# Decoder trunk on one core: seeded banks at feed-forward ends, the last tile on ScalarE, later gains

## What is computed

```python
h = LN(ALPHA * h + 0.5 * swiglu(h, ffn_a))     # gate and up 1024 x 2816, down 2816 x 1024
h = LN(ALPHA * h + mixer(h))                   # three groups of heads, one projection in, one out
h = LN(ALPHA * h + 0.5 * swiglu(h, ffn_b))
# swiglu(x) = (silu(x @ w_gate) * (x @ w_up)) @ w_down;  LN(x) = (x - mean) * rsqrt(var + eps) * g + b
```

## Time and profile before

| | |
|---|---|
| runs | 1899.64, 1900.06, 1900.58 us |
| median | 1900.06 us |
| the profiled execution's own time | 1899.35 us |
| its span, first to last instruction | 1897.6 us |
| mean granted TensorE clock | 0.998 of full speed |
| busy: TensorE, VectorE, ScalarE, GpSimd | 98%, 74%, 39%, 11% |

### The profile page before, as it was taken

How to read it: one execution, slowest core, us unless ns; L and a number is a source line. 1 busy time by engine, 2 the same in 40 slices (tenths; PEclk the granted TensorE clock), 3 DMA queues, 4 the chain that set the end, 5 groups by cost and what they waited for, 6 DMA issues and landing times.

```text
span 1897.6 us, 25000 instructions
## 1 busy us (share of the span) xinstructions
PE 1867.6 (98%) x9121; PEld 1572.7 (83%) x9121; DVE 1411.4 (74%) x2059; ACT 741.0 (39%) x1114; POOL 217.0 (11%) x247
## 2 busy tenths in 40 slices
PE   7999999999999999999999999999999999999998
PEld 6888888889888888888888888888888888888886
DVE  7877877952676878787897777777536688777777
ACT  5332333434554423333253242423455543424243
POOL 2000000153323000000100000003343220000001
PEclk9999999999999999999999999999999999999999
DMA  5222223236742222222313222223557323222221
GB/s 215 100 111 88 111 88 133 91 119 179 207 115 90 111 88 111 88 111 88 133 69 131 89 111 88 111 111 107 153 156 210 89 83 115 111 88 111 88 111 45
DMA packets 43747, 215.95 MB, mean 114 GB/s; under 512 B 8756, under 2 KB 11252, under 8 KB 20008
## 3 DMA queue, kind: packets, MB, share of 16 engines
q1 hardware_dynamic: 40808, 199.30, 29.7%
q0 software_dynamic: 2880, 15.90, 3.6%
HBM read 197.23 MB, written 17.93 MB: 113 GB/s over the span
## 4 chain that ended last, share of the span: by engine, by line
PE 90%; DVE 5%; issue 2%; ACT 1%; DMA 1%; POOL 1%; SPq 0%; ACTq 0%; DVEq 0%; POOLq 0%
PE psum L1011 80%; PE psum L1216 5%; PE psum L1313 2%; DVE res L1540 1%; PE psum L1303 1%; PE psum L1042 1%; PE psum L1291 1%; DVE st L1557 1%; DVE negm L1898 1%; DVE xlo L1496 0%; DMA gbc<-in_gb_col 0%; PE psum L1415 0%; PE psum L1242 0%; POOL rstd L609 0%; ACT psum L919 0%
## 5 line engine op out<-in xcount | busy, mean ns | idle before, releaser
L1011 PE MATMUL psum<-xhi,whiA 128*128 128x512 f32 (+1 forms) x768 | 287.4, 374 | 4.9 <-DVE xlo L1496 4.9
L1011 PE MATMUL psum<-xlo,whiA 128*128 128x512 f32 (+1 forms) x768 | 285.9, 372 | 0.0
L1011 PE MATMUL psum<-xhi,wloA 128*128 128x512 f32 (+1 forms) x768 | 285.8, 372 | 0.0
L1011 PE MATMUL psum<-xhi,whiB 128*128 128x512 f32 x704 | 273.9, 389 | 0.0
L1011 PE MATMUL psum<-xlo,whiB 128*128 128x512 f32 x704 | 273.9, 389 | 0.0
L1011 PE MATMUL psum<-xhi,wloB 128*128 128x512 f32 x704 | 273.9, 389 | 0.0
L1011 PE MATMUL psum<-whiD,hl 128*128 128x512 f32 x768 | 264.0, 390 | 2.0 <-DVE wloD L1473 2.0
L799 ACT ACTIVATE s<-psum 128x512 f32<-128x512 f32 x40 | 23.9, 598 | 540.7 <-PE psum L1011 540.6
L1651 DVE SCALAR_TENSOR_TENSOR res<-psum,res 128x1024 f32<-128x1024 f32 x120 | 146.7, 1222 | 82.1 <-PE psum L1011 82.1
L1651 DVE SCALAR_TENSOR_TENSOR nat<-psum,nat 128x1024 f32<-128x1024 f32 x144 | 175.8, 1221 | 26.3 <-PE psum L1011 26.3
L1011 PEld LDWEIGHTS psum<-xhi,whiA 128*128 128x128 f32 x768 | 145.4, 189 | 32.4 <-DVE xlo L1496 6.0
(11 more groups left out here) (230 smaller groups left out, 3520.5 us busy)
## 6 DMA issues: line engine op xcount, KB each, us to landing
rawA<-in_a_w SPq DMA_DIRECT2D x62, 1024.0 KB, 6.3
rawB<-in_b_w SPq DMA_DIRECT2D x54, 1024.0 KB, 4.8
rawD<-in_d_w SPq DMA_DIRECT2D x46, 1024.0 KB, 4.7
stacks<-hl SPq DMA_DIRECT2D x192, 64.0 KB, 1.7
whiD<-stacks POOLq DMA_DIRECT2D x10, 768.0 KB, 6.4
wloD<-stacks POOLq DMA_DIRECT2D x10, 768.0 KB, 5.9
gbr<-in_gb_row SPq DMA_DIRECT2D x6, 1024.0 KB, 8.4
stacks<-wloD SPq DMA_DIRECT2D x48, 64.0 KB, 1.7
```

The lines of the kernel that those rows point to most:

```text
L1011: ins = t_.matmul(out_, a_, b_, start=(start and k == 1), stop=(stop and k == n), skip_group_check=check)
```

## The change

1. At the end of a feed-forward stage ScalarE copies tiles 0 and 1 of `res` into banks 4 to 7 (the seeds), and the products of the first four output halves are added on top of them (start is off). VectorE adds nothing there: it takes the statistics from the banks, and ScalarE normalises tiles 0 and 1 from the banks. The other four halves go to banks 2, 3, 2, 3 and are added to `res` as before. So that the banks need no factor, h is scaled by 0.5 as it is split. `y_free` counts four additions at such an end (`freed`).
2. Fold 4 is cut in two: the two additions that finish tiles 0 and 1 stand ahead of the split of D, the two others where all four stood.
3. After a feed-forward stage tiles 0 and 1 are turned into banks 4 to 7, and tiles 2 and 3 too.
4. At all five joints ScalarE normalises tile 3, behind its split of B; VectorE's `last_tile` inside `turn` goes.
5. At all five joints VectorE does three half-chunks ahead of the last addition and three behind it (BEGUN = 6), and only then the last statistics. With 4, its half-chunks 6 and 7, the last subtraction and the low part of B follow the aggregate directly.
6. In the first seven-product of a stage the gains of tiles 1 to 3 all move behind the low part of the sums of D (tlo).
7. The output stage swaps the two groups of banks.

```diff
-OUT_BANKS = [(0, 1, 2, 3), (4, 5, 6, 7)]
+OUT_BANKS = [(4, 5, 6, 7), (0, 1, 2, 3)]
...
+BEGUN = 6
+SEED_BANKS = (4, 5, 6, 7)
+SEEDED = 4
+FFN_BANK = [4, 5, 6, 7, 2, 3, 2, 3]
+Y_ADDS = (8 - SEEDED, 8, 8 - SEEDED)
...
+        def freed(y):
+            l, i = divmod(y, Y_ALL)
+            return 4 + l * sum(Y_ADDS) + sum(Y_ADDS[:i])
+        def after_ffn(q):
+            return q > 0 and q % 3 != 2
+        def half_banks(q, h):
+            return SEED_BANKS if after_ffn(q) else HALF_BANKS[h]
...
                         act.wait_ge(y_done, y * 8 + AHEAD)
                         split("B", b_fill)
+                        act.wait_ge(nmr_ok, NT * q + NT)
+                        a.activation(nat[:, NT - 1, :], res[:, NT - 1, :], ACT.Identity, bias=nmr[:, NT - 1:NT],
+                                     scale=rstd[:, NT - 1:NT]).then_inc(zd_ok, 1)
...
+                    if after_ffn(q) and t < 2:
+                        a.activation(nat[:, t, :].rearrange("p (a n) -> p a n", a=2), psum[:, 4 + 2 * t:6 + 2 * t, :], ACT.Identity,
+                                     bias=nmr[:, t:t + 1], scale=rstd[:, t:t + 1]).then_inc(za_ok, 1)
...
-                    a.activation(hhi["A"], h32["A"], ACT.Copy).then_inc(hhi_ok["A"], 1)
+                    a.activation(hhi["A"], h32["A"], ACT.Copy, scale=0.5).then_inc(hhi_ok["A"], 1)
+                    act.wait_ge(fold_ok, (2 * l + f) * 8 + 6)
+                    for t in range(2):
+                        a.activation(psum[:, 4 + 2 * t:6 + 2 * t, :], res[:, t, :].rearrange("p (a n) -> p a n", a=2),
+                                     ACT.Copy).then_inc(seed_ok, 1)
...
+                if after_ffn(q) and h == 1:
+                    pe.wait_ge(y_free, freed(y))
...
+                        if after_ffn(q) and h == 0:
+                            if (t, i) == (0, 2):
+                                pe.wait_ge(za_ok, 3 * q + 2)
...
-                    if n == 0:
-                        pe.wait_ge(y_free, y * 8 + o + 1)
-                    ins = product(bank[4 + o % 4][:, :], [(stat(t), w(slot, off + hf * 512, 512))],
-                                  start=(n == 0), stop=(n == 1))
+                    if n == 0 and o < SEEDED:
+                        pe.wait_ge(seed_ok, y // Y_ALL * 4 + (2 if y % Y_ALL else 0) + t + 1)
+                    elif n == 0 and o >= 6:
+                        pe.wait_ge(y_free, freed(y) + o - 5)
+                    ins = product(bank[FFN_BANK[o]][:, :], [(stat(t), w(slot, off + hf * 512, 512))],
+                                  start=(n == 0 and o >= SEEDED), stop=(n == 1), check=o < SEEDED)
...
-                        if q and h == 0 and c == 5:
-                            dve.wait_ge(rstd_ok, NT * q + NT)
-                            last_tile(q)
...
+                    if o < seeded:
+                        dve.wait_ge(y_done, y * 8 + o + 1 + AHEAD)
+                        summed = bank[FFN_BANK[o]][:, :]
+                    else:
+                        dve.wait_ge(y_free, freed(y) + o - seeded + 1)
+                        summed = res[:, t, hf * 512:hf * 512 + 512]
+                    v.bn_stats(st[:, t, hf, :], summed).then_inc(st_ok, 1)
...
+                if seeded:
+                    for o in range(4):
+                        stats(o)
...
+                stats(late - 1)
+                for c in range(3):
+                    half_chunk(q + 1, 0, c)
+                for o in range(late, 8):
+                    add(y, o)
+                for c in range(3, BEGUN):
+                    half_chunk(q + 1, 0, c)
+                for o in range(late, 8):
+                    stats(o)
...
+                    fold(4)
                     split("D", l * D_ALL + f * D_FFN2 + i)
...
-                    v.tensor_tensor(hlo["A"], h32["A"], f32(hhi["A"]), ALU.subtract).then_inc(h_ok["A"], 1)
-                    fold(4)
+                    v.scalar_tensor_tensor(out=hlo["A"], in0=h32["A"], scalar=0.5, in1=f32(hhi["A"]), op0=ALU.mult,
+                                           op1=ALU.subtract).then_inc(h_ok["A"], 1)
+                    fold(5)
...
+                    elif k == 4:
+                        dve.wait_ge(m_free, (q + 1) * SEVENS * 7 + AHEAD)
+                        add_to(c12, m6, 3)
+                        add_to(c11, m1)
                     else:
                         add_to(m7, m5)
-                        dve.wait_ge(m_free, (q + 1) * SEVENS * 7 + AHEAD)
-                        add_to(c12, m6, 3)
-                        add_to(c22, m7, 5)
-                        add_to(c11, m1)
+                        add_to(c22, m7, 7)
...
-                    if begin:
-                        gain(1)
-                        gain(2)
...
-                    if begin:
-                        gain(3)
                     split("D", d)
                     dve.wait_ge(thi_ok, n + 1)
                     v.tensor_tensor(tlo, tsum, f32(thi[:, :]), ALU.subtract).then_inc(tlo_ok, 1)
+                    if begin:
+                        for t in range(1, NT):
+                            gain(t)
```

More of the change, by code:

```diff
@@ L749, in normalise @@
                     act.wait_ge(nmr_ok, NT * q + t + 1)
-                    a.activation(nat[:, t, :], res[:, t, :], ACT.Identity, bias=nmr[:, t:t + 1],
-                                 scale=rstd[:, t:t + 1]).then_inc(za_ok, 1)
+                    if after_ffn(q) and t < 2:
+                        a.activation(nat[:, t, :].rearrange("p (a n) -> p a n", a=2), psum[:, 4 + 2 * t:6 + 2 * t, :], ACT.Identity,
+                                     bias=nmr[:, t:t + 1], scale=rstd[:, t:t + 1]).then_inc(za_ok, 1)
+                    else:
+                        a.activation(nat[:, t, :], res[:, t, :], ACT.Identity, bias=nmr[:, t:t + 1],
+                                     scale=rstd[:, t:t + 1]).then_inc(za_ok, 1)
             def ffn(l, f):
@@ L784, in last_pair @@
                         a.activation(hhi["B"][:, h * 256:h * 256 + 256], h32["B"][:, h * 256:h * 256 + 256],
-                                     ACT.Copy).then_inc(hhi_ok["B"], 1)
+                                     ACT.Copy, scale=0.5).then_inc(hhi_ok["B"], 1)
                 def gather(n, k):
@@ L1032, in turn_z @@
                     for i in range(NT):
[L1033 to L1036 removed]
+                        b = half_banks(q, h)[i]
+                        if after_ffn(q) and h == 0:
+                            if (t, i) == (0, 2):
+                                pe.wait_ge(za_ok, 3 * q + 2)
+                        elif not after_ffn(q) and t == 0 and (b >= 6 or h == 0 and b >= 4):
+                            pe.wait_ge(y_free, freed(y) + b - 7)
                         elif t == 0 and h == 1:
@@ L1561, in stats @@
                         v.bn_aggr(mv[:, t, :], st[:, t, :, :].rearrange("p a n -> p (a n)")).then_inc(mv_ok, 1)
[L1563 to L1570, removed]
+                if seeded:
+                    for o in range(4):
+                        stats(o)
+                else:
+                    for o in range(4):
+                        add(y, o)
+                        if o >= 1:
+                            stats(o - 1)
+                    stats(3)
                 for o in range(4, late):
-                    add(y, o, scale)
+                    add(y, o)
                     if o >= 5:
                         stats(o - 1)
[L1575 to L1579, removed]
-                        add(y, o, scale)
-                        half_chunk(q + 1, 0, 2 + o - late)
-                    for c in range(2 + HELD, 4):
-                        half_chunk(q + 1, 0, c)
-                    for o in range(late, 8):
-                        stats(o)
-                else:
-                    stats(7)
+                if ends:
+                    stats(7)
+                    return
+                stats(late - 1)
+                for c in range(3):
+                    half_chunk(q + 1, 0, c)
+                for o in range(late, 8):
+                    add(y, o)
+                for c in range(3, BEGUN):
+                    half_chunk(q + 1, 0, c)
+                for o in range(late, 8):
+                    stats(o)
             def ffn(l, f):
-                turn(3 * l + 2 * f, l * B_ALL + f * B_FFN2, 4 if l + f else 0)
+                turn(3 * l + 2 * f, l * B_ALL + f * B_FFN2, BEGUN if l + f else 0)
                 if (l, f) == (0, 0):
@@ L1613, in last_pair @@
                         dve.wait_ge(hhi_ok["B"], n * 2 + h + 1 + AHEAD)
-                        v.tensor_tensor(hlo["B"][:, t], h32["B"][:, t], f32(hhi["B"][:, t]), ALU.subtract).then_inc(h_ok["B"], 1)
+                        v.scalar_tensor_tensor(out=hlo["B"][:, t], in0=h32["B"][:, t], scalar=0.5, in1=f32(hhi["B"][:, t]),
+                                               op0=ALU.mult, op1=ALU.subtract).then_inc(h_ok["B"], 1)
                 def gain(t):
```

31 lines of the change are left out of this document (18 added, 13 removed).

## The result

The changed kernel takes **1906.81 us** (median of 8 runs, 1903.85 to 1909.68) beside 1900.16 for the kernel before. The ratio is 1.0036, with a 95% interval of 1.0025 to 1.0047: slower, and 2.8 us above the upper end of the predicted range. One of the eight executions of the kernel before took 3119.34 us; it counts in the median and not in the ratio, which is of fast runs alone. The profiled execution is one of the quicker ones, 1905.41 us with a span of 1903.7. Its span is 6.1 us above that of before, where the prediction's sum said 1.6.

A forecast was written before the change was run, and what follows sets the result against it. TensorE, busy 98% of the span, was taken as the bound; -0.62 + 0.5 + 0.6 + 1.96 - 0.87 = +1.6 us gave 1900.9 profiled, 1901.6 as a median, with a range of 1892 to 1904.

The forecast's parts named there:

- the end of the joint after a feed-forward stage: Tile 3's transposes and seventh chunk of x: chunk at 376.15 against 375.95, loss 0.2 us, three times.
- last pair: Last two products of h in a stage: second half of h comes later, cost 0.12 us each, 0.5 for four.
- The forecast's mechanism: At the joints GpSimd's last operation asks 0.14 us after VectorE's split of B starts, and waits until 373.92.
- The mixer joints: Two joints after a mixer: chunk at 607.33 against 606.35, loss 0.98 us each, 1.96 in all.
- The tail: End of the kernel: last aggregate at 1887.6 against 1888.47, gain 0.87 us.
- The first products: First stage: the wait for wloD goes, ScalarE's first gather is late next; gain 0.62 us, once.
- The seeds: Two ScalarE copies per stage, taken at 1.05 us each, in idle time; no cost even at 2.0.
- The race the other way: Rival, chance 0.20: after a feed-forward stage GpSimd asks before the split of B; 1.8 us gained three times, 1895.6.
- The whole hold by GpSimd: Rival, chance 0.15: GpSimd's rstd holds VectorE's reads for its whole length, so nmr precedes the split of B; 1892.6.
- The cast that I held against this rival: Sign against GpSimd holding reads: a cast at 366.59 kept its 0.29 us during rstd at 366.43.
- The lost handover: Rival, chance 0.10: waiting GpSimd can't get between VectorE's instructions, rstd waits for the split's end; 0.7 more per joint, 1905.1.
- My slower rival: At five joints VectorE's queue wins over GpSimd's older request; 0.7 us more each, 1905.1, chance 0.10.

The follow-up runs named there:

- run 2: Changed kernel plus nine products nobody reads ahead of TensorE's wait for tile 3 at all five joints; 1901.31 us, ratio 1.001.
- run 12: Changed kernel plus the nine unread products at the two joints after a mixer only; 1904.28 us, ratio 1.0027.
- run 11: Changed kernel plus the nine unread products at the three joints after a feed-forward stage only; 1902.27 us, ratio 1.002.
- run 1: Changed kernel plus one wait: VectorE starts its split of B at a joint only when nmr is done; 1891.08 us, ratio 0.9955.

## Why the prediction was wrong

**The step that failed is the end of the joint after a feed-forward stage**: "ScalarE 374.0 to 375.25, the tile's transposes at 375.3, and the chunk 0.85 later". The 0.85 is a duration at 2.4 GHz, and I carried it behind a wait of 2.7 which the kernel before has nowhere at a joint. The granted clock was never asked for there; it stood at 1.00 in all I read. Nothing in the sum, the rivals or the range has a term for it. In the profiled execution it costs 1.39, 1.57 and 1.54 at the three joints, measured against run 2 (4.50). Joint and last pair together cost 0.21, 0.18 and 0.18 in run 2, where the prediction had 0.32, so without the clock the sum was near. The 4.50 are as large as the missing 4.5 in part by luck: the rest of the ledger misses too, -0.97 at the start against +1.10 in the mixers and +0.25 at the end.

The timed runs pay more: their mean clock is 0.995 or 0.996 in seven of eight, the profiled one's is 0.997, and one fall is 3.41 us at half speed in 1904, 0.0009 of the mean. Run 2, with the same tail, has 0.999 or 1.000 in all ten. The mean is a rough counter, though: one execution of run 12 shows 0.972 at 1906.29 us, only 2 above its median. Run 2 measures the term in the timed runs, 5.5 us (4.9 by the ratios), and run 11's profile shows that a joint after a mixer can pay it as well.

The Trainium skill, "TensorE: Matmul & The Clock Gate", "What's actually happening", states that a gate passes either 1.2 or 2.4 GHz to the array, by how busy TensorE has been recently. The trace agrees: 0.50 and 1.00 are the levels of the stretches above, with the wait between them.

The kernel before had shown the sign, and I quoted the row in front of it without reading on. TensorE and then the granted clock in the tail of the kernel **before**:

```profile
1889.41 1.09 PE L1453 MATMUL psum<-ident,nat 128*128 128x128 f32 x8 [2.12 <-DVE nat L1971]
1890.94 1.97 PE L1453 MATMUL psum<-ident,nat 128*128 128x128 f32 x8 [0.45 <-DVE nat L1971]
```

```profile
1886.00:1890.60 4.60, 2.38 (x20) 1.91 (x18) 3.79 (x10) 3.78 (x9) 2.73 (x8) 1.00 0.22 73
1890.60:1893.00 2.40, 1.97 (x8) 1.57 (x8) 1.54 (x4) 0.90 (x2) 0.34 (x1) 0.51 0.90 300
```

After a wait of 2.12 and a second of 0.45 the last eight transposes take 1.97 instead of 1.09, at 0.51. A price for a wait of that length stood in the trace; the sum should have carried it as an unknown of the forecast, from 0 to some 0.9 for eight transposes and more for what follows them, five times.

**The forecast's mechanism was right, to two tenths.** Ahead of the first joint TensorE is 1.33 earlier than before, so I add that to the after-times. Aggregate: predicted 370.0, measured 369.84. Split of B: 371.64 and 371.48. nmr's end: 373.92 and 373.82. Transposes: 375.3 and 375.15. The race was lost by 0.14, as said, and it was lost at all five joints: by 0.13 to 0.15 after a feed-forward stage, by 0.30 after a mixer (0.29 predicted).

**The mixer joints**: 0.98 predicted, 1.02 and 0.94 measured. **The last pairs**: 0.12, measured 0.09 to 0.17. **The tail**: 0.87, measured 0.92. **The first products**: 0.62 predicted, 0.49 measured; the next wait is the one named, ScalarE's first gather:

```profile
46.27 0.50 PE L1043 MATMUL psum<-whiD,hl 128*128 128x512 f32 x1 [1.45 <-ACT nat L824]
```

**The seeds**: 1.05 assumed, 0.98 measured (two in 1.96). Both are done at 351.18, the first product of h starts at 352.42, and none waits for them. ScalarE:

```profile
349.22 1.96 ACT L807 ACTIVATE psum<-res 128x1024 f32<-128x1024 f32 x2
```

**The rivals.** The race the other way, priced 6.0 us under the forecast (1895.6), is what run 1 forces at a small cost to VectorE, and it came to 1891.1, 10 below run 2. The joints after a feed-forward stage give 2.0 each in the two profiles, as priced. The rest comes from the two after a mixer, 1.85 each: the wait for nmr keeps the split off there as well, where I had it blocking in either outcome. The whole hold by GpSimd is refuted: while rstd runs, from 369.41 to 370.15, two subtractions with two SBUF inputs take 0.42 each (0.75 together, from 369.32), and the split starts at 370.15, when ScalarE's part of it is in (368.17 and 1.95). The cast that I held against this rival has only one SBUF input and said nothing of such a subtraction. The Trainium skill's page "SBUF — State Buffer", "Who interferes with whom", has whoever starts first keep the shared pair and the other block. Of VectorE's split the trace agrees (nmr 2.20 instead of 0.19); of GpSimd's small rstd it doesn't. The lost handover is refuted too: rstd takes 0.74 between VectorE's subtractions, and doesn't wait for the split. My slower rival had the wrong mechanism; its side came true by luck, through the clock.

**What stays open.** 1.10 us arise inside the two mixers of the changed kernel's profile (0.41 and 0.69). Run 2, which differs by the idle products alone, has 0.06 and -0.39 there. In the twelve runs' profiles the first mixer lies between 0.02 and 1.11 and the second between -0.57 and 0.26, and the change's 0.69 is the highest. One execution of each can't tell how much of this is scatter and how much belongs to the change. Nor do the runs say why a wait of 2.5 to 2.7 lets the clock fall at one joint and not at the next: in the profiles of the change and of runs 11 and 12 there are ten such waits and six falls. Fewer than nine idle products weren't tried.

## What to carry to other kernels

When a change leaves TensorE one long wait in place of several short ones, price the products behind it at 1.2 GHz as well, and look at the granted clock by stretch, since forty slices of a page don't show 3.4 us. Ask of each small GpSimd operation on the path which long VectorE instruction with two SBUF inputs can start just ahead of it; a wait on VectorE, or one step of work between, is cheaper than losing the race. Parts that gain alone must be timed together: here two gains made a race, and the place of one half-chunk decided some 16 us.

## What the runs showed of the hardware that I had not expected

TensorE's clock fell to 1.2 GHz around waits of 2.5 to 2.7 us, six times in ten, and at no joint whose waits were 0.83 or less; each fall lasted 3.41 us and cost 1.4 to 1.6 us. In the change's first joint it fell already 0.4 before the work came back (373.42, work at 373.82), and in the five other falls between 0.15 before and 0.70 after. Behind the wait of 2.12 in the tail of before it fell at 1890.63 only, in the short wait ahead of the last eight transposes. Kept busy with nine useless products, it didn't fall. The runs of the change scatter most: 1903.85 to 1909.68 in 8, 5.8 us, beside 4.5 and 3.9 in the 11 each of runs 11 and 12, 2.3 in the 10 of run 2, and 3.6 at most in the runs without such a wait.
